# Value slabs in pairs with 512 moving columns, query and key slabs ahead of them, in an fp32 transformer trunk

## What is computed

```python
# layer 1: x (256 x 1024), w_in (1024 x 3072)
proj = rmsnorm(x, g_mix) @ w_in
sb_q, sb_k, sb_v, da_q, da_k, da_v = split(proj)      # 512 columns each
o_a = stick_breaking_attention(sb_q, sb_k, sb_v)      # 8 heads of 64
q1, q2, k1, k2 = (partial_rope(rmsnorm(h)) for h in halves(da_q, da_k))
o_b = rmsnorm((softmax(q1 k1^T) - lam * softmax(q2 k2^T)) @ da_v)   # 4 heads of 2 x 64
gates = sigmoid(rmsnorm(x, g_mix) @ w_gate + b_gate)  # then merged, w_out, feed-forward
# layer 2: forgetting attention, 16 heads of 64
q, k, v, f = split(rmsnorm(h, g) @ fox_w_in)          # 1024, 1024, 1024, 16 columns
o = softmax(q k^T / 8 + decay(cumsum(log_sigmoid(f)))) @ v
# layer 3: latent attention with shared keys and values, then feed-forward
```

## Time and profile before

| | |
|---|---|
| median of three runs | 1010.24 us (1009.67 to 1011.06) |
| span of the profiled execution | 1007.6 us |
| TensorE matmul busy | 993.9 us, 99% |
| VectorE busy | 714.1 us, 71% |
| ScalarE busy | 607.8 us, 60% |
| GpSimd busy | 59.6 us, 6% |
| mean granted TensorE clock | 0.997 of full speed |

### The profile page before, as it was taken

One profiled execution on the slowest core, in us unless ns is written; L12 is line 12 of the kernel. 1 busy time (PEld: TensorE's weight loads), 2 busy tenths in 40 slices (PEclk: granted clock), 3 DMA queues, 4 the chain that ended last, 5 costly groups with the idle time before them and its releaser, 6 DMA issues.

```text
span 1007.6 us, 19765 instructions
## 1 busy us (share of the span) xinstructions
PE 993.9 (99%) x7214; PEld 923.4 (92%) x7214; DVE 714.1 (71%) x1360; ACT 607.8 (60%) x1094; POOL 59.6 (6%) x79
## 2 busy tenths in 40 slices
PE   8999999999999999999999999999999999999997
PEld 8999989999999999989999999999989999999996
DVE  4668987776666668666496666668977686666665
ACT  5677785575555556565475555557768675555553
POOL 3011110120000002000020000002200010000000
PEclk9999999999999999999999999999999999999999
DMA  7743445466555554433545556564665456565631
GB/s 292 273 149 110 153 145 187 148 206 190 176 181 186 183 189 159 157 127 127 167 146 188 187 187 187 187 187 127 203 194 191 146 167 188 187 187 187 187 125 43
DMA packets 50904, 174.05 MB, mean 173 GB/s; under 512 B 6304, under 2 KB 8864, under 8 KB 50720
## 3 DMA queue, kind: packets, MB, share of 16 engines
q1 hardware_dynamic: 49664, 172.12, 52.9%
q10 hardware_dynamic: 1184, 1.18, 0.6%
HBM read 169.86 MB, written 1.05 MB: 170 GB/s over the span
## 4 chain that ended last, share of the span: by engine, by line
PE 90%; DVE 5%; ACT 2%; DMA 1%; issue 1%; SPq 0%; DVEq 0%; ACTq 0%
PE bank L426 89%; DVE w_lo L1485 2%; PE bank L647 1%; DVE a_pair L1504 1%; DMA stage<-slab_dram 1%; DVE xT L1515 1%; DVE arena L1478 0%; ACT w_hi L1032 0%; ACT a_pair L1067 0%; DVE soft_s L1566 0%; ACT soft_p L1124 0%; ACT w_hi L1016 0%; DVE tmp L1478 0%; DVE tmp L1712 0%; DVE arena_r L1485 0%
## 5 line engine op out<-in xcount | busy, mean ns | idle before, releaser
L426 PE MATMUL bank<-a_pair,w_hi 128*128 128x256 f32 (+1 forms) x1992 | 537.8, 342 | 2.8 <-DVE w_lo L1485 2.7
L426 PE MATMUL bank<-a_pair,w_lo 128*128 128x256 f32 x1488 | 417.6, 282 | 0.0
L1485 DVE TENSOR_TENSOR w_lo<-stage,w_hi 128x1024 fp32r<-128x1024 f32 (+2 forms) x322 | 387.4, 1211 | 8.4 <-ACT w_hi L1016 3.5
L426 PEld LDWEIGHTS bank<-a_pair,w_hi 128*128 128x128 f32 x1992 | 343.4, 190 | 48.6 <-DVE w_lo L1485 4.0
L426 PE MATMUL bank<-arena_r,w_hi 128*128 128x256 f32 x1792 | 328.8, 284 | 0.4 <-DVE arena_r L1485 0.2
L426 PEld LDWEIGHTS bank<-arena_r,w_hi 128*128 128x128 f32 x1792 | 278.4, 191 | 5.6 <-DVE arena_r L1485 1.4
L426 PEld LDWEIGHTS bank<-a_pair,w_lo 128*128 128x128 f32 x1488 | 283.1, 190 | 0.0
L426 PE MATMUL bank<-arena_r,w_lo 128*128 128x256 f32 x896 | 252.7, 283 | 0.0
L1016 ACT ACTIVATE w_hi<-stage 128x1024 fp32r<-128x1024 f32 x192 | 202.4, 1055 | 33.4 <-PE bank L426 33.4
L1032 ACT ACTIVATE w_hi<-stage 128x1024 fp32r<-128x1024 f32 (+2 forms) x126 | 128.0, 1026 | 79.5 <-PE bank L426 69.7
L426 PEld LDWEIGHTS bank<-arena_r,w_lo 128*128 128x128 f32 x896 | 171.0, 191 | 0.0
(11 more groups left out here) (185 smaller groups left out, 674.8 us busy)
## 6 DMA issues: line engine op xcount, KB each, us to landing
stage<-slab_dram SPq DMA_DIRECT2D x319, 512.0 KB, 4.2
con<-con_dram SPq DMA_DIRECT2D x1, 1153.5 KB, 10.6
xT<-xT_dram SPq DMA_DIRECT2D x4, 256.0 KB, 5.5
arena<-arena ACTq DMA_DIRECT2D x1, 1024.0 KB, 8.9
arena<-tmp SPq DMA_DIRECT2D x32, 32.0 KB, 3.2
out_dram<-arena SPq DMA_DIRECT2D x3, 256.0 KB, 2.4
tmp<-arena SPq DMA_DIRECT2D x16, 16.0 KB
vec<-vec_dram SPq DMA_DIRECT2D x1, 213.5 KB, 11.5
```

The costliest lines, as they stand in the source:

```text
L426: return nc.tensor.matmul(out, lhsT, rhs, start=start, stop=True, skip_group_check=True)
L1485: return nc.vector.tensor_tensor(out, a, hi.bitcast(f32), ALU.subtract)
```

## The change

Groups of queries, keys and values are no longer interleaved as 4 + 2. The loads follow `QKV_ORDER`: in SB the order is 4 query/key, 4 value, 4 query/key slabs; in DA it is 8 query/key, then 4 value slabs; in each half of FOX it is 4, 4, 4 and 2, 4, 6. Four value slabs are two pairs. A pair holds the same half of the contraction for two blocks of 256 value columns, and `values_in` multiplies both slabs at once: the moving operand is 2 x 256 columns out of two slots, the output is a whole bank for each half of the tokens. A pair's first half handles tokens 0 to 127, its second half tokens 128 to 255; `slab_done` rises by 2 at the end. ScalarE copies values out once for four slabs, as two copies of 512 columns. Banks change: values use banks 4 and 5 in SB and 2 and 3 elsewhere, query/key slabs banks 0 to 3, the norm sums of the first pair bank 4. The norm sums of the second differential pair stand behind DA+10 and DA+11, beside the value slabs, instead of behind GATE+0 and GATE+1; its factors, key scaling, swap and rotation move with them. `FOX_AT` moves the last three starts one or two slabs later. Nothing else changes in what is computed.

```diff
+QKV_ORDER = {"plain": (0, 1, 2, 3, 4, 10, 5, 11, 6, 7, 8, 9), "diff": (0, 1, 2, 3, 6, 7, 8, 9, 4, 10, 5, 11),
+             "fox0": (0, 2, 1, 3, 4, 10, 5, 11, 6, 8, 7, 9), "fox1": (0, 2, 4, 10, 5, 11, 1, 3, 6, 8, 7, 9)}
-FOX_AT = {FOX + s: k for k, s in enumerate((6, 8, 10, 12, 15, 17, 21, 23))}
+FOX_AT = {FOX + s: k for k, s in enumerate((6, 8, 10, 12, 15, 19, 22, 24))}
-        QK_BANK, V_BANK = (4, 0, 1, 2), 3
+        def v_bank(S, t):
+            return bank[(2 if S else 4) + t]
         def qk_half(J, c):
-            if J > 4 and c == 0:
-                return half(2, 1)
-            return half(QK_BANK[c], 0)
+            return half((4, 0, 1, 3)[c] if J == 4 else c, 0)
+        def qkv_role(n):
+            first = next(at for at in (FOX + 12, FOX, DA, SB) if n >= at)
+            S, c = (SB, DA, FOX, FOX + 12).index(first), n - first
+            v_at = (4, 8, 4, 2)[S]
+            if v_at <= c < v_at + 4:
+                return "v", S, c - v_at
+            J, c = divmod(c if c < v_at else c - 4, 4)
+            return "qk", 2 * S + J, c
...
-                if n - GATE in (3, 6, 9, 11):
-                    swap_halves(*((0, 0), (1, 0), (0, 1), (1, 1))[(3, 6, 9, 11).index(n - GATE)])
+                if n - GATE in (3, 6, 9, 10):
+                    swap_halves(*((0, 0), (1, 0), (0, 1), (1, 1))[(3, 6, 9, 10).index(n - GATE)])
...
+            def qkv_slab(n, m):
+                kind, J, c = qkv_role(n)
+                if kind == "v":
+                    values_in(J, c, n)
                     return
-                pe.wait_ge(lo_made, n + 1)
-                if J and c == 4:
-                    pe.wait_ge(v_taken, J)
-                if J == 3 and c == 4:
-                    pe.wait_ge(q_factor, 1)
+                if J:
+                    pe.wait_ge(qk_taken, 4 * J + c - 3)
+                if J in (5, 6) and c >= 2:
+                    pe.wait_ge(v_taken, J - 2)
...
+            def values_in(S, i, n):
+                e, t = divmod(i, 2)
+                if t == 0:
+                    pe.wait_ge(lo_made, n + 2)
+                if e == 0 and S:
+                    pe.wait_ge(qk_taken, (0, 16, 20, 24)[S] + t - 1)
+                slots = slice((n - t) % SLOTS, (n - t) % SLOTS + 2)
                 for k in range(4):
                     w = slice(k * TOK, (k + 1) * TOK)
-                    for t in range(2):
-                        x = (slice(None), 4 * (c - 4) + k, slice(t * P, t * P + P))
-                        last = by_tokens(w_hi[:, slot, w], w_lo[:, slot, w], half(V_BANK, t), a_hi[x], a_lo[x],
-                                         c == 4 and k == 0 and t == 0)
-                last.then_inc(slab_done, 1)
+                    x = (slice(None), 4 * e + k, slice(t * P, t * P + P))
+                    last = by_tokens(w_hi[:, slots, w], w_lo[:, slots, w],
+                                     v_bank(S, t).rearrange("p (j n) -> p j n", j=2), a_hi[x], a_lo[x],
+                                     e == 0 and k == 0)
+                if t:
+                    last.then_inc(slab_done, 2)
...
+            for n in range(DA, GATE):
+                qkv_slab(n, 0)
+                if n in (DA + 6, DA + 8, DA + 10, DA + 11):
+                    da_norm_sum((DA + 6, DA + 8, DA + 10, DA + 11).index(n))
+                attend(n)
             for c in range(16):
                 n = GATE + c
                 if c >= 2:
                     pe.wait_ge(g_taken, c - 1)
+                elif c:
+                    pe.wait_ge(v_taken, 2)
                 else:
-                    pe.wait_ge(qk_taken, 16)
+                    pe.wait_ge(q_factor, 1)
                 column_slab(n, n % SLOTS, half(GATE_BANK[c % 2], 0))
-                if c < 2:
-                    da_norm_sum(2 + c)
                 attend(n)
...
-                     lambda c: (o_lo, c + 1), free={0: (qk_taken, 32), 6: (v_taken, 8)})
+                     lambda c: (o_lo, c + 1), free={2 * i: (qk_taken, 29 + i) for i in range(4)})
...
+            def v_out(n):
+                kind, S, i = qkv_role(n)
+                if kind != "v" or i != 3:
+                    return
+                v, at = ((sb_v, 0), (da_v, 0), (fox_v, 0), (fox_v, 512))[S]
                 act.wait_ge(slab_done, n + 1)
+                act.wait_ge(col_ready, 1 if S < 2 else 2)
                 for t in range(2):
-                    last = nc.scalar.activation(v[:, t, j * TOK:(j + 1) * TOK], half(V_BANK, t), ACT.Copy,
+                    last = nc.scalar.activation(v[:, t, at:at + 512], v_bank(S, t)[:, :], ACT.Copy,
                                                 scale=r_col[:, t:t + 1])
...
+                if n == DA + 10:
+                    pair_squares(2)
+                if n == DA + 11:
+                    keys_factor(1)
+                    pair_squares(3)
...
             for c in range(16):
                 n = GATE + c
-                if c == 1:
-                    keys_factor(1)
-                if c < 2:
-                    pair_squares(2 + c)
                 if c and c % 2 == 0:
                     gates_out(c - 2)
+                if c == 0:
+                    queries_factor(1)
                 next_hi(n)
-                if c == 2:
-                    queries_factor(1)
                 attend(n)
...
                 if n == DA + 8:
                     normed_keys(0)
+                if n == DA + 11:
+                    normed_keys(1)
...
-                if c == 1:
-                    normed_keys(1)
                 if c == 2:
+                    da_probs(0)
                     partners(0, 1)
-                    da_probs(0)
-                if c == 5:
+                if c == 3:
                     partners(1, 1)
...
                 attend(n)
-                if c == 5:
+                if c == 3:
                     rotated(0, 1)
                     rotated(1, 1)
```

## The result

The changed kernel takes **1029.31 us** (median of 5 runs, 1028.81 to 1032.97) against 1010.24 before (1009.67 to 1011.06): ratio 1.020, 95% interval 1.019 to 1.021: slower by about 2%. The forecast was 1028.7. The execution that was profiled is the longest of the five: span 1031.2 us at a mean granted clock of 0.987, where the other four have spans of 1027.1 to 1028.4 at 0.992 to 0.994. So some 3 to 4 us of what this trace shows are not in the median.

A forecast was written before the change was run, and what follows sets the result against it. TensorE's queue was taken to bound the kernel. Waits of 18.65 less 1.7 saved plus 1.5 of clock, on a span of 1007.6 with 2.6 around it, gave 1028.7 us; range 1019 to 1034.

The forecast's parts named there:

- What bounds the kernel: Whole kernel: TensorE, busy 99% of the span, sets the end; savings and waits there count one for one.
- (b): Behind DA+9, differential values: TensorE waits for both heads' masked exponentials behind ScalarE's blocked split; 2.9 us, up to 3.7.
- (d): Behind DA+11, differential values: TensorE waits for `keys_factor(1)` and `pair_squares(3)`, both behind the blocked split; 3.1 us.
- (h): Behind FOX+17: `turned(9)` waits 1.65 us for a copy; then FOX+18 waits 1.0 more for the value copy.
- The saving: Value slabs: 192 matmuls of 512 columns replace pairs of 256, saving TensorE 1.7 us.
- the nearer row: Latent attention's value slab before the change: 512-column matmuls, each after a weight load, take 0.231 us each.
- (c): Behind DA+10, differential values: the moved norm sum waits for `pair_squares(2)` behind `sb_log(3)`; 1.0 us.
- The pair argument: Value pairs: late release blocks ScalarE's split, so TensorE requests queued behind it wait 1.2 us plus the thing itself.
- The clock: Behind the long waits in both attention blocks: TensorE drops to 1.2 GHz; 1.5 us taken, between nothing and 3.9.
- every long wait costs the clock: Rival, whole kernel: 512s save nothing, long waits bring slow clock, mask and gates at upper ends; 1036.1 us, chance 0.10.
- half of it is absorbed: Rival, whole kernel: ScalarE and VectorE catch up during waits, and one wait swallows the next; 1019 us, chance 0.10.
- The pairs block nothing: Rival, value pairs: ScalarE's split is off the path, leaving the two gains alone; 1006.7 us, chance 0.05.

The follow-up runs named there:

- squares and rotation: Kernel with splits behind the attend steps, plus the DA+10 squares one slab earlier on ScalarE and VectorE's gate rotation spread out: 1009.59 us.

## Why the prediction was right, point by point

**What bounds the kernel** held behind the start: what was taken out of TensorE's waits came out of the time. The runs with splits behind, with squares and rotation, and with all waits gone took off 16.0, 3.75 and 2.3 us. The last two removed waits of 3.5 and 2.1. The first removed 14.0 (the six at (b), (d) to (h) below) and uncovered 1.8 and 0.5 (before FOX+18); the other 4 or so are left for the slow clock that is gone, which is what remains and was not measured by itself.

**The saving** held: 1.7 said, 1.2 to 1.5 measured as a difference of two kernels. The pair's matmuls step by 0.23, two of them from 27.05 to 27.51, here in the first pair of the kernel after:

```profile
27.05 0.62 PE L439 MATMUL bank<-w_hi,a_pair 128*128 128x512 f32 x2
27.51 0.40 PE L439 MATMUL bank<-w_lo,a_pair 128*128 128x512 f32 x1
```

That is the step of the nearer row of before. The 131 ns that the Trainium skill gives for sustained 512s (page "TensorE: Matmul & The Clock Gate", section "Back-to-back issue gap") would, as an estimate, have made the pairs win by some 21 us; the run with pairs of 256 shows 1.5 at most, so this case doesn't bear the figure out.

**The waits,** said and measured (idle time in the trace of after, 0.16 added behind a matmul of 512):

| place | said | measured |
|---|---|---|
| start, low halves of slabs 5 and 7 | 0.3 + 0.75 | 0 + 0.5 |
| (a) second bank, DA+8 | 0.15 | nothing to be seen |
| (b) DA+9, mask | 2.9 | 2.6 |
| (c) DA+10, squares | 1.0 | 0, behind a slow stretch |
| (d) DA+11, factor and squares | 3.1 | 3.06 |
| gates, net of the 1.8 that went | 0.8 | 0.5 |
| (e) FOX+5, `f_ready` | 1.95 | 1.9 |
| (f) FOX+7, turn of head 0 | 2.9 | 2.97 |
| (g) FOX+15, `outputs(3)` | 1.65 | 1.7 |
| (h) FOX+17, turn, then the value copy | 1.65 + 1.0 | 1.8 + 0.6 |
| (i) FOX+19, scores | 0.5 | 0.5 |
| latent attention, one turn | none | 0.55 |

Together 18.65 said, 16.7 measured. The pair argument held at every place that it named a wait of over 1 us: ScalarE's timeline shows it for (d) as it was worked out, the split right behind the pair's end, then `keys_factor(1)` and `pair_squares(3)`:

```profile
97.94 1.06 ACT L1043 ACTIVATE w_hi<-stage 128x1024 fp32r<-128x1024 f32 x1 [3.25 <-PE bank L439]
98.91 0.67 ACT L1047 ACTIVATE tmp<-bank,con 128x512 f32<-128x512 f32 x1
...
100.14 0.61 ACT L1320 ACTIVATE sq<-arena 128x512 f32<-128x512 f32 x1
```

Each answers to its row of before. The biggest miss among the terms is (c): I had written that a slow clock behind (b) would hide it, and still counted it at its full 1.0. The run with the rotation spread out, where the slow stretch lay a little earlier and the clock was full again from 91.0, shows a wait of 0.76 there. The 1.8 of the run with the splits behind is not this wait, since one more split is in it.

**The clock** was the term that I undersized: 1.5. The windows of the kernel after, each inside the stretch behind a wait (columns as above; the seventh number is the granted clock):

```profile
89.50:92.80 3.30, 3.30 (x13) 2.50 (x10) 1.28 (x3) 2.68 (x6) 0.00 (x0) 0.50 0.13 51
103.20:106.40 3.20, 3.20 (x17) 3.20 (x17) 0.89 (x1) 0.83 (x4) 1.41 (x2) 0.50 0.10 19
430.90:437.50 6.60, 5.97 (x29) 5.75 (x29) 3.44 (x7) 3.25 (x8) 0.00 (x0) 0.50 0.48 154
478.60:481.90 3.30, 3.30 (x17) 3.30 (x17) 0.00 (x0) 1.02 (x2) 0.00 (x0) 0.50 0.56 182
...
131.50:134.60 3.10, 3.10 (x27) 3.10 (x28) 2.82 (x4) 2.98 (x6) 0.00 (x0) 1.00 0.30 95
```

1.2 GHz behind (b), (d), (f) and (h), against the one stretch at the start before; full clock behind the second turn. In this execution the first value slab starts at 22.48, 1.3 later than before, for the granted clock is still 0.50 from 10.9 to 14.2, where it was 0.94 before. The same code got there at 22.63 in the run with the norm back in the gates and at 21.58 in the one with the rotation spread out. So it is luck and not the change. The accounts of the two attention blocks leave for the clock: 10.3 - 1.3 - (0.5 + 2.6 + 3.06 + 0.5) + 0.9 saved = 3.2, and 12.9 - 9.5 + 0.9 saved = 4.3. So 7.5 behind the waits and 1.3 at the start in the profiled execution, where 1.5 were said. The usual execution has a span of about 1027.5; if its waits are the same, 1007.6 + 16.7 - 1.7 leaves 4.9 of clock there, as an estimate.

The row from which I priced a slow stretch was also read wrongly. I took 1.3 us as lost behind the start, since 13 matmuls took 2.90 us and not 1.56. The run with the late release in the kernel before has the same code there and ran it at full clock:

```profile
7.60:10.90 3.30, 2.63 (x18) 2.26 (x18) 2.38 (x6) 2.26 (x6) 0.00 (x0) 1.00 1.04 407
...
11.83 0.50 PE L426 MATMUL bank<-a_pair,w_hi 128*128 128x256 f32 x2 [1.03 <-DVE w_lo L1486]
```

It reached its first value slab at 21.28, no earlier than the 21.21 of before: at full clock TensorE waited for low halves instead. A slow stretch that short costs next to nothing there. What one costs where TensorE sets the pace is not in that row; by the account above, the two behind (b) and (d) cost 3.2 together, 1.6 each.

A third term was off: I put 2.6 around the span. In every execution since, the time is 1.7 to 1.9 above the span (1032.97 and 1031.2 here); the rest of the 2.6 was, by that, that the profiled execution of before was some 0.85 faster than its median.

So the mechanism was right, and that the total came out to 0.6 us was luck, by misses that offset each other: the waits 1.95 too high, the clock 3.4 too low, and the time around the span 0.85 too high. The rival "every long wait costs the clock" (1036.1) was the closer one on the clock, and its other terms were too high. The rival "half of it is absorbed" described (c) alone. "The pairs block nothing" fell at the first row of waits, and the runs show what it would have taken: with the splits behind the attend steps, and the other waits removed, the kernel takes 1007.3, which is the 1006.7 of that rival but for small waits.

## What to carry to other kernels

When two slabs are merged into one unit, look at who waits for the first slab's release and what is queued behind that wait on an engine that takes its work in order. The cost was not in the merged matmuls: moving the split copies behind their neighbours in ScalarE's queue gave back 16 of 19 us, with the pairs, their order and their late release untouched. And price such a wait by the whole list of steps that the consumer has between the slab and the request: a pair of scores ahead of a turn left 0.59 us of idle time where 1.65 of waiting had been counted.

While TensorE has long waits, one execution can differ from the next by 5 us with the same instructions, so a small edit is to be timed after the long waits are gone and not before.

## What the runs showed of the hardware

The slow level is not a fixed function of the idle time ahead of it. The kernel after has a granted clock of 0.50 in its window from 430.90, around the end of the wait of 2.81 us at 431.53. In the run with the splits first in the forgetting part:

```profile
419.54 0.55 PE L668 MATMUL bank<-con,soft_p 128*128 128x128 f32 x3 [2.81 <-DVE soft_p L1664]
...
419.50:422.90 3.40, 3.37 (x29) 3.23 (x29) 2.87 (x5) 2.67 (x5) 0.00 (x0) 1.00 0.37 113
```

the same turn with the same 2.81 us of idle time ahead of it went on at 2.4 GHz. In the run with the splits first in the differential part the wait of 2.42 was followed by full clock and the one of 2.90 by the slow level:

```profile
86.20:89.50 3.30, 3.25 (x23) 2.60 (x24) 0.42 (x1) 3.04 (x6) 0.00 (x0) 1.00 0.47 163
99.10:102.30 3.20, 3.20 (x16) 3.20 (x16) 2.42 (x3) 1.63 (x5) 1.44 (x2) 0.50 0.40 147
```

A wait of 2.10 had it behind it in the run with single values and one of 2.11 hadn't in the kernel after. Shorter waits can have it behind them too: in the run with the late release in the kernel before, waits of 1.57 and 0.74 ended at 437.24 and 438.85, and behind them stands

```profile
438.50:441.70 3.20, 2.85 (x14) 2.86 (x15) 2.24 (x7) 2.70 (x7) 0.00 (x0) 0.50 0.23 64
```

while the same 1.57 at (g) in the kernel after had none. So a wait of 1.6 to 3 us costs itself, and in some executions the slow level for what follows; what decides between the two, these traces don't show. Six executions of the kernel with the splits first in the differential part spread from 1013.58 us (mean clock 0.998) to 1018.75 (0.990). The Trainium skill, page "TensorE: Matmul & The Clock Gate", section "What's actually happening", says that the number of slow matmuls at a kernel's start varies from run to run, because the gate keeps its own time. The start agrees (0.50 from 8.2 to 11.2 in the kernel before, 1.00 from 7.6 to 10.9 in the run with the late release, which has the same code there), and these runs show the same of waits in the middle of a kernel.
